# An up projection fed with x times the norm's weight, 1/rms applied at eviction, norms by logarithm, and paired fillers in a triangular inverse

## The chip, the cores and the metric

The kernel runs on one core of one Trainium2 chip. The metric is device time in microseconds of one execution of the whole step, and the median of several timed runs counts. Beside them one execution was profiled; all rows below come from that one.

## The reference, cut to what matters

One layer of a hybrid decoder is applied to 1040 prompt rows (16 learned meta tokens and 1024 prompt tokens) and 8 decode rows; the kernel carries them together as 1050 columns (two are padding). All inputs are float32.

```
def rms_norm(x, g):
    xf = x.astype(jnp.float32)
    y = xf * lax.rsqrt(jnp.mean(xf * xf, axis=-1, keepdims=True) + RMS_EPS)
    return (y * g.astype(jnp.float32)).astype(x.dtype)
...
    h = rms_norm(x, lw['norm_mix'])
    u = h @ lw['w_in']
...
    merged = jax.nn.sigmoid(g_r) * (o_r @ lw['w_br_rwkv']) + jax.nn.sigmoid(g_f) * (o_f @ lw['w_br_fox'])
    x = x + merged @ lw['w_out']
    h2 = rms_norm(x, lw['norm_ffn'])
    x = x + jnp.square(jax.nn.relu(h2 @ lw['w_ffn_up'])) @ lw['w_ffn_down']
...
    y_prompt = rms_norm(xp[:, N_META:], norm_final)
```

Between `u` and `merged` stand a recurrent branch (RWKV-7: per head a 64x64 state with a delta rule, run over time) and an attention branch with a forget bias (FoX). D_MODEL is 1024, the MLP is 4096 wide, and there are 8 heads of 64 in each branch.

## The kernel before

**Layout.** The residual x lies transposed in SBUF as 8 tiles of 128 features by 1050 columns (`XT`, k = 0 to 7). A projection makes one tile of 128 output features at a time, in three PSUM banks of 350 columns; this is called a unit here. Units alternate between slot s = 0 (banks 0 to 2) and s = 1 (banks 3 to 5), and banks 6 and 7 are left to others. Two units are a pair `v`, and its weights are loaded by SyncE into `W[:, s]`.

**Split units** (`pe_unit_split`, L273 to L286). The RWKV input projection, the branch, out, up and down projections multiply in two parts of each operand: high (rounded to float32r, by ScalarE) and low (the remainder, by VectorE). Each k needs nine matmuls (high by high, high weight by low x, low weight by high x, three banks each), so a unit has 72. ScalarE makes a unit's high weights (`act_split`, L288), VectorE its low ones (`dve_split`, L296). A unit waits for its weights, for the emptying of its slot (`evac[s]`), and, if it is given `ready`, for each k of its input.

**RMS norms** (n = 0 before the input projection, 1 before the MLP, 2 at the end). ScalarE squares a tile (L307 to L313), VectorE adds the squares up (L320 to L325), TensorE sums over partitions with three float32 matmuls by ones into banks 0 to 2 (`pe_norm`, L300), ScalarE takes the square root of all 1050 columns (`act_rms`, L315), VectorE the reciprocal (`dve_rms`, L327), and then VectorE makes each normed tile as x times weight times 1/rms (`normed`, L331). For norms 0 and 1 ScalarE and VectorE then split the tile into high and low, and the next projection waits tile by tile. For norm 2 each of the eight tiles is stored by its own DMA, in order (L784 to L786).

**The RWKV chunks.** Ten chunks of 104 columns run one after the other (`pe_chunk`). In a chunk TensorE follows an order written out by hand. It inverts a triangular matrix per head by doubling, in levels 1 to 6 (`LEVELS`, L954 to L998). Level by level: products `t1` (banks 0 and 1, both half-sets q of four heads), ScalarE copies them to `T1`, products `t2` (for each q first X times T1 into bank 2 + q, then T1 times X transposed into bank 4 + q), and VectorE subtracts these from `Xm` (L1734) and `XTr` (L1737). GpSimd meanwhile makes the next levels' masked operands (L2099). The products are 64-row or 40-row tiles, each float32 matmul being two instructions. Between these steps stand fillers (`Filler`, L334 to L352): full 128x128 float32 matmuls, two instructions each, of the FoX and gate projections. 48 fillers belong to a chunk; in the inverse one stands after `t1` and one after `t2`.

**The MLP.** Four chunks of 8 up units and 8 down units. After an up unit ScalarE empties the slot with Relu, VectorE squares, ScalarE makes the high and VectorE the low part (`act_up` L1556, `dve_up` L2051). After an out or down unit VectorE adds the banks to `XT` (`residual`, L2015 to L2020).

**Queues.** Each engine works through its instructions in order, so an instruction that waits holds all behind it; SyncE's DMA issues likewise.

## Time and profile before

| | us |
|---|---|
| median of three timed runs (2258.6 to 2265.17) | 2263.16 |
| the profiled execution | 2257.22 |
| its span, first to last instruction | 2255.4 |
| TensorE busy in it | 2101.6 (93%) |
| VectorE busy | 920.3 (41%) |
| ScalarE busy | 592.5 (26%) |
| GpSimd busy | 191.8 (9%) |

The profile lists instructions by engine (PE is TensorE's matmuls, PEld its weight loads, DVE is VectorE, ACT ScalarE, POOL GpSimd, SP SyncE) and source line. A row of the timeline is start, duration, engine, line, operation, tiles, shapes, count, and in brackets the idle time of the engine before it with what ended it. A busy TensorE is not TensorE at its peak: where matmul records overlap, the distance of their starts counts. The stretches of the execution are: norm 0 (to 64 us), RWKV input projection (to 227), preparation (to 288), ten chunks of 64.8 us each (to 925), rest of the fillers and attention (to 1260), branch and out projections (to 1458), norm 1 (to 1493), MLP (to 2226), norm 2 and the stores (to 2255).

### The profile page before, as it was taken

How to read it: one execution, taken by the hardware profiler on the slowest of the kernel's cores; microseconds unless marked ns; L12 is line 12 of the kernel's file. 1: busy time of each engine (PE TensorE's matmuls, PEld its weight loads, DVE VectorE, ACT ScalarE, POOL GpSimd, SP SyncE). 2: the span in 40 equal slices, each digit the busy share in tenths (PEclk: the TensorE clock that was granted, in tenths of full speed). 3: DMA queues.
4: the chain of work that ended last, by engine and by line, in shares of the span. 5: the costliest groups of instructions: out<-in, count | busy, mean ns of one | idle time of the engine just before them, and what ended most of it. 6: DMA issues, size and time to landing. Idle time of an engine off the chain costs nothing.

```text
span 2255.4 us, 42657 instructions
## 1 busy us (share of the span) xinstructions
PE 2101.6 (93%) x17388; PEld 1800.3 (80%) x17388; DVE 920.3 (41%) x1448; ACT 592.5 (26%) x955; POOL 191.8 (9%) x186
## 2 busy tenths in 40 slices
PE   2999899999999999998999899979999999999995
PEld 1999477777777777655566899879999999999994
DVE  5433534444433344341877663362223223212334
ACT  3213422222222222212544651232112102101210
POOL 0000022222122222001210000000000000000000
PEclk8999899999999999999999999989999999999998
DMA  3122511111102221565646362101111111111111
GB/s 119 39 84 76 222 38 48 47 47 47 37 25 55 55 66 43 143 123 183 206 167 211 132 219 94 37 29 46 47 47 46 47 46 37 46 46 46 46 37 76
DMA packets 104545, 180.96 MB, mean 80 GB/s; under 512 B 59886, under 2 KB 60206, under 8 KB 102342
## 3 DMA queue, kind: packets, MB, share of 16 engines
q1 hardware_dynamic: 102118, 170.65, 23.1%
q10 hardware_dynamic: 2304, 8.50, 1.6%
q8 instruction: 99, 1.62, 0.3%
q14 instruction: 24, 0.20, 0.0%
HBM read 145.58 MB, written 33.54 MB: 79 GB/s over the span
## 4 chain that ended last, share of the span: by engine, by line
PE 81%; DVE 8%; DMA 4%; SPq 2%; ACT 2%; issue 2%; DVEq 0%; ACTq 0%
PE ps L284 46%; PE ps L350 18%; PE ps L903 4%; PE ps L904 3%; DMA weights<-in_wu 2%; DVE arena L1713 1%; SPq L731 1%; DMA normed<-in_vp 1%; SPq L737 1%; PE ps L1020 1%; DVE normed L332 1%; PE ps L1142 1%; PE ps L1025 1%; PE ps L943 1%; PE ps L1013 1%
## 5 line engine op out<-in xcount | busy, mean ns | idle before, releaser
L350 PE MATMUL ps<-normed,weights 128*128 128x350 f32 x1344 | 446.3, 474 | 5.0 <-DMA weights<-in_wu 4.2
L284 PE MATMUL ps<-h_split,w_split 128*128 128x350 f32 x2304 | 374.9, 325 | 15.6 <-DVE h_split L2039 15.6
L284 PEld LDWEIGHTS ps<-h_split,w_split 128*128 128x128 f32 x2304 | 373.1, 190 | 17.8 <-issue 12.9
L284 PE MATMUL ps<-ff_split,w_split 128*128 128x350 f32 x2304 | 371.4, 323 | 0.0
L284 PEld LDWEIGHTS ps<-ff_split,w_split 128*128 128x128 f32 x2304 | 370.9, 189 | 0.0
L350 PEld LDWEIGHTS ps<-normed,weights 128*128 128x128 f32 x1344 | 243.2, 191 | 126.5 <-issue 14.3
L903 PEld LDWEIGHTS ps<-arena 64*64 64x64 f32 x2400 | 148.6, 135 | 46.1 <-issue 26.5
L2020 DVE TENSOR_TENSOR arena<-arena,ps 128x1050 f32 (+1 forms) x40 | 50.0, 1249 | 328.1 <-PE ps L284 328.1
L2099 POOL TENSOR_TENSOR arena<-arena,constants 64x512 f32<-64x512 f32 x120 | 132.5, 1105 | 445.6 <-DVE arena L1713 378.8
L903 PE MATMUL ps<-arena 64*64 64x64 f32 x2400 | 163.7, 220 | 1.0
L904 PE MATMUL ps<-arena 40*40 40x64 f32 x2400 | 157.5, 218 | 0.0
L294 ACT CAST w_split<-weights 128x1024 fp32r<-128x1024 f32 x78 | 81.3, 1043 | 276.8 <-PE ps L284 245.1
L284 PE MATMUL ps<-h_high,w_split 128*128 128x350 f32 x672 | 135.3, 334 | 15.4 <-DVE h_low L1593 15.4
L2055 DVE TENSOR_TENSOR squares<-squares 128x1050 f32<-128x1050 f32 x32 | 40.1, 1253 | 248.5 <-ACT squares L1561 248.5
L904 PEld LDWEIGHTS ps<-arena 40*40 40x40 f32 x2400 | 138.8, 112 | 0.0
L284 PEld LDWEIGHTS ps<-h_high,w_split 128*128 128x128 f32 x672 | 114.4, 192 | 19.9 <-issue 13.9
L298 DVE TENSOR_TENSOR w_split<-weights,w_split 128x1024 fp32r<-128x1024 f32 x78 | 95.1, 1219 | 78.3 <-ACT w_split L294 78.3
L1734 DVE TENSOR_TENSOR arena<-arena,ps 104x256 f32<-104x256 f32 (+1 forms) x100 | 41.9, 419 | 190.3 <-PE ps L904 184.2
L1561 ACT ACTIVATE squares<-ps 128x1050 f32<-128x1050 f32 x32 | 33.5, 1048 | 259.5 <-PE ps L284 259.5
L1411 ACT COPY arena<-ps 104x256 f32<-104x256 f32 (+1 forms) x120 | 44.6, 372 | 160.1 <-PE ps L904 116.0
L1862 DVE CUSTOM_DVE_ANT_0 arena<-ps,arena 104x416 f32<-104x416 f32 (+3 forms) x152 | 67.7, 492 | 36.6 <-PE ps L1187 36.6
L284 PE MATMUL ps<-mg_high,wb_split 128*128 128x350 f32 x384 | 73.9, 328 | 5.2 <-DVE wb_split L298 5.2
(282 smaller groups left out, 2424.7 us busy)
## 6 DMA issues: line engine op xcount, KB each, us to landing
weights<-in_wu SPq DMA_DIRECT2D x122, 512.0 KB, 3.5
normed<-in_vp SPq DMA_DIRECT2D x64, 260.0 KB, 4.5
normed<-in_kp SPq DMA_DIRECT2D x64, 256.0 KB, 4.9
arena<-chunk_dram SPq DMA_DIRECT2D x10, 1248.0 KB, 6.9
arena<-gate_dram SPq DMA_DIRECT2D x16, 525.0 KB, 4.0
chunk_dram<-arena SPq DMA_DIRECT2D x12, 520.0 KB, 4.0
chunk_dram<-fox SPq DMA_DIRECT2D x12, 520.0 KB, 3.8
arena<-samp_dram SPq DMA_DIRECT2D x10, 512.0 KB, 9.2
```

Of the source, the lines that this page charges most:

```text
L284: last = pe.matmul(PS[:, 3 * s + g, 0:G], ws[s][wh][:, k * P:(k + 1) * P], x[xh][:, k, g * G:(g + 1) * G], start=(k == 0 and wh + xh == 0) ...
L294: act.copy(of[0][s][0], W[:, s]).then_inc(w_hi[s], 1)
L298: dve.tensor_tensor(of[0][s][1], W[:, s], of[0][s][0], ALU.subtract).then_inc(w_split[s], 1)
L350: last = self.pe.matmul(PS[:, 6 + m % 2, 0:G], W[:, s, k * P:(k + 1) * P], HT[:, k, g * G:(g + 1) * G], start=(k == 0), stop=(k == KT - 1))
L903: pe.matmul(PS[top, bank, at], a[top], b[top], start=True, stop=True)
L904: return pe.matmul(PS[low, bank, at], a[low, 0:HR], b[low], start=True, stop=True)
L1411: ch_act.done(act.copy(quad(T1, q)[part], PS[part, q, 0:4 * HB]), f"t1_{lv}_{q}")
L1734: done(dve.tensor_tensor(quad(Xm, q)[part], quad(Xm, q)[part], PS[part, 2 + q, 0:4 * HB], ALU.subtract), f"x_{lv}_{q}_x")
L1862: dve.tensor_tensor_reduce(Sm[u % 3][0:C, e, lo:hi].rearrange("p b t -> p (b t)"), PS[0:C, 2 * (n % 2) + e, (lo - CUTS[c][0]) * C:(hi - CU ...
L2020: dve.tensor_tensor(dst, dst, grp(s), ALU.add).then_inc(evac[s], 1)
L2055: dve.tensor_tensor(RL[s], RL[s], RL[s], ALU.mult).then_inc(ff_raw, 1)
L2099: ch_pool.done(pool.tensor_tensor(Bm[lv % 2][part, :, 0:n], MB[part, :, 0, part], mask.unsqueeze(1).to_broadcast([n, NH, n]), ALU.mult), f ...
```

## The change

**Norms.** `act_rms` takes the logarithm group by group (three instructions of 350 columns, the weight 1/D and the epsilon in it), and then one exponential of -0.5 times it over 1050 columns; that is 1/rms, and VectorE's reciprocal goes. `pe_norm` signals after each of its three groups; norms 0 and 1 write banks 6 and 7 (group 2 waits until group 0 is read), norm 2 banks 0 to 2.

**Norm 1 and the MLP.** As soon as an out tile k is added to `XT`, ScalarE writes `HS[0][k]`, the high part of x times the norm's weight, and VectorE the low part. The first up unit follows the last out unit directly; the three sums over partitions are put into it, two groups ahead of its k = 5 and one ahead of k = 7. 1/rms is applied where an up unit is emptied, by VectorE (maximum with 0, times 1/rms), then ScalarE squares and makes the high part, and VectorE the low part. ReLU and the scale commute, because 1/rms is positive. Buffers of the split operands move to other places.

**Norm 2.** VectorE makes tiles 0 to 5. ScalarE multiplies tiles 6 and 7 of `XT` by the weight ahead of time, and GpSimd multiplies them by 1/rms. The stores are issued in the order 0, 1, 6, 2, 3, 7, 4, 5.

**Inverse.** The products that change X get a signal of their own (`t2x`) and come first for both q, then the other products; VectorE subtracts in that order. The next level's `t1` waits for X alone, and `t2x` for X transposed. The two fillers of a level stand together between `t1` and `t2`.

```diff
@@ pe_norm, act_rms, dve_rms
-        def pe_norm(pe, n):
+        def norm_out(n, g):
+
+            return PS[:, g if n == 2 else 6 + g % 2, 0:G]
+
+        def pe_norm(pe, n, groups=range(NG)):
             sqsum = norms[n][1]
-            pe.wait_ge(sq_added, KT * (n + 1))
-            for g in range(NG):
-                last = pe.matmul(PS[:, g, 0:G], ones, sqsum[:, g * G:(g + 1) * G], start=True, stop=True)
-            last.then_inc(ssum_ready, 1)
+            for g in groups:
+                pe.wait_ge(sq_added, KT * (n + 1))
+                if g == 2 and n < 2:
+                    pe.wait_ge(rms_ready[n], 1)
+                pe.matmul(norm_out(n, g), ones, sqsum[:, g * G:(g + 1) * G], start=True, stop=True)\
+                  .then_inc(ssum_ready[n], 1)
...
-            act.wait_ge(ssum_ready, n + 1)
-            act.activation(g3(norms[n][2]), grp(0), ACT.Sqrt, scale=1.0 / D,
-                           bias=par[:, V_EPS:V_EPS + 1]).then_inc(rms_ready, 1)
+            rstd = norms[n][2]
+            for g in range(NG):
+                act.wait_ge(ssum_ready[n], g + 1)
+                act.activation(rstd[:, g * G:(g + 1) * G], norm_out(n, g), ACT.Ln, scale=1.0 / D,
+                               bias=par[:, V_EPS:V_EPS + 1]).then_inc(rms_ready[n], 1)
+            act.wait_ge(rms_ready[n], NG)
+            act.activation(rstd, rstd, ACT.Exp, scale=-0.5).then_inc(rms_ready[n], 1)
...
-            dve.wait_ge(rms_ready, n + 1)
-            order(dve.reciprocal(norms[n][2], norms[n][2]))
+            dve.wait_ge(rms_ready[n], NG + 1)
@@ sync: the stores
-            for k in range(KT):
-                sp.wait_ge(h_ready, 2 * KT + k + 1)
+            for k in (0, 1, 6, 2, 3, 7, 4, 5):
+                if k < N_DVE:
+                    sp.wait_ge(h_ready, 2 * KT + k + 1)
+                else:
+                    sp.wait_ge(out_made, k - N_DVE + 1)
                 sp.dma_start(A["o_y"][:, k, :], HT[:, k, :]).then_inc(out_stored, 16)
@@ tensor: the inverse
-                            wait(ch_dve, f"x_{lv - 1}_{q}_xt")
+                            wait(ch_dve, f"x_{lv - 1}_{q}_x")
...
-                    fill.run(1)
+                    fill.run(2)
                     for q in range(2):
                         wait(ch_act, f"t1_{lv}_{q}")
+                        if lv > 1:
+                            wait(ch_dve, f"x_{lv - 1}_{q}_xt")
...
+                        ch_pe.done(last, f"t2x_{lv}_{q}")
+                    for q in range(2):
                         for j in range(4):
                             last = by_halves(4 + q, j, T1, XTr, 4 * q + j)
                         ch_pe.done(last, f"t2_{lv}_{q}")
-                    fill.run(1)
@@ tensor: the MLP's start
-            pe.wait_ge(evac[0], V_FF0 - PV_FILL)
-            pe_norm(pe, 1)
-            pe.wait_ge(rms_ready, 2)
-            pe_unit_split(pe, V_FF0, 0, halves(HS), lambda k: pe.wait_ge(h_ready, KT + 1 + k))
-            pe_unit_split(pe, V_FF0, 1, halves(HS))
+            def summed(k):
+                pe.wait_ge(h_ready, KT + 1 + k)
+                if k == 5:
+                    pe_norm(pe, 1, (0, 1))
+                if k == 7:
+                    pe_norm(pe, 1, (2,))
+
+            pe_unit_split(pe, V_FF0, 0, HS, summed)
+            pe_unit_split(pe, V_FF0, 1, HS)
@@ scalar: out projection, up units, the end
+            for k in range(KT):
+                j, s = divmod(k, 2)
+                act_split(act, j + (V_OUT0 + 1), s, of=BRO)
+                act.wait_ge(evac[s], j + (V_OUT0 - PV_FILL + 1))
+                act.activation(HS[0][:, k], XT[:, k, :], ACT.Identity,
+                               scale=par[:, V_NF + k:V_NF + k + 1]).then_inc(h_hi, 1)
+                act_square(act, 1, k, s)
             act_rms(act, 1)
...
-                        act.activation(g3(RL[s]), grp(s), ACT.Relu).then_inc(evac[s], 1)
                         act_split(act, KT * c + j + (V_FF0 + 1), s)
+                        act.wait_ge(evac[s], KT * c + j + (V_FF0 - PV_FILL + 1))
+                        act.activation(RL[s], RL[s], ACT.Square).then_inc(ff_raw, 1)
...
+                    if 2 * j + s >= N_DVE:
+                        k = 2 * j + s
+                        act.wait_ge(sq_ready, 2 * KT + k + 1)
+                        act.activation(XT[:, k, :], XT[:, k, :], ACT.Identity, scale=par[:, V_NL + k:V_NL + k + 1])\
+                           .then_inc(out_scaled, 1)
@@ vector: out projection, up units, the end
+            for k in range(KT):
+                j, s = divmod(k, 2)
+                residual(j, k + (2 * V_OUT0 + 1), s)
+                dve_split(dve, j + (V_OUT0 + 1), s, of=BRO)
                 dve.wait_ge(h_hi, k + 1)
+                dve.scalar_tensor_tensor(HS[1][k], XT[:, k, :], par[:, V_NF + k:V_NF + k + 1],
+                                         HS[0][:, k].bitcast(F32), ALU.mult, ALU.subtract).then_inc(h_ready, 1)
+                dve_add_square(dve, 1, k, s)
+            dve_rms(dve, 1)
...
-                        dve.tensor_tensor(RL[s], RL[s], RL[s], ALU.mult).then_inc(ff_raw, 1)
+                        dve.scalar_tensor_tensor(g3(RL[s]), grp(s), 0.0, rstd1, ALU.max, ALU.mult)\
+                           .then_inc(evac[s], 1)
...
-            for k in range(KT):
+            for k in range(N_DVE):
                 normed(dve, 2, k, V_NL, HT[:, k, :]).then_inc(h_ready, 1)
@@ gpsimd: the end
+            pool.wait_ge(rms_ready[2], NG + 1)
+            for k in range(N_DVE, KT):
+                pool.wait_ge(out_scaled, k - N_DVE + 1)
+                pool.tensor_tensor(HT[:, k, :], XT[:, k, :], norms[2][2], ALU.mult).then_inc(out_made, 1)
```

## Rows read from the trace of the kernel before

**Rows 1.** The page: busy time by engine, and the chain that ended last, by engine.
```profile
PE 2101.6 (93%) x17388; PEld 1800.3 (80%) x17388; DVE 920.3 (41%) x1448; ACT 592.5 (26%) x955; POOL 191.8 (9%) x186
...
PE 81%; DVE 8%; DMA 4%; SPq 2%; ACT 2%; issue 2%; DVEq 0%; ACTq 0%
```
**Rows 2.** The waits of TensorE: us in total, times, longest.
```profile
PE ps L304 <- DVE arena L325: 35.3, 2, 31.5
PE ps L284 <- DVE h_split L2039: 15.6, 5, 11.9
```
**Rows 3.** The timeline of norm 0: ScalarE's root, VectorE's reciprocal and next step.
```profile
35.33 1.14 ACT L317 ACTIVATE arena<-ps,params 128x1050 f32<-128x1050 f32 x1 [3.39 <-PE ps L304]
36.50 6.72 DVE L329 RECIPROCAL arena<-arena 128x1050 f32<-128x1050 f32 x1 [5.19 <-ACT arena L317]
43.25 1.22 DVE L298 TENSOR_TENSOR w_split<-weights,w_split 128x1024 fp32r<-128x1024 f32 x1
```
**Rows 4.** The timeline of ScalarE in a chunk: a 350-column bank, Ln, Exp's table.
```profile
657.52 0.45 ACT L363 COPY fox<-ps 128x350 f32 x1 [3.21 <-PE ps L350]
...
663.05 0.30 ACT L1420 ACTIVATE arena<-arena,params 104x8 f32<-104x8 f32 x1 [3.77 <-DVE arena L1771]
663.37 1.28 ACT L1423 ACT_TABLE_LOAD   x1
```
**Rows 5.** The timeline of TensorE in the inverse: four fillers, then level 1's single ones.
```profile
620.36 2.62 PE L350 MATMUL ps<-normed,weights 128*128 128x350 f32 x8
622.91 0.27 PE L903 MATMUL ps<-arena 64*64 64x64 f32 x1
...
625.98 0.27 PE L903 MATMUL ps<-arena 64*64 64x64 f32 x1
...
627.78 0.28 PE L903 MATMUL ps<-arena 64*64 64x64 f32 x2
627.99 0.86 PE L350 MATMUL ps<-normed,weights 128*128 128x350 f32 x2
628.77 0.27 PE L903 MATMUL ps<-arena 64*64 64x64 f32 x1
```
**Rows 6.** The timeline of VectorE at the same place: its first subtraction of level 1.
```profile
627.18 0.42 DVE L1734 TENSOR_TENSOR arena<-arena,ps 104x256 f32<-104x256 f32 x1 [7.32 <-PE ps L904]
```
**Rows 7.** The timeline around norm 1: last out tile, first up unit, its emptying.
```profile
1457.73 1.25 DVE L2020 TENSOR_TENSOR arena<-arena,ps 128x1050 f32<-128x1050 f32 x1 [7.96 <-PE ps L284]
...
1476.77 7.18 PE L284 MATMUL ps<-h_split,w_split 128*128 128x350 f32 x27 [11.94 <-DVE h_split L2039]
...
1496.09 1.05 ACT L1561 ACTIVATE squares<-ps 128x1050 f32<-128x1050 f32 x1 [3.46 <-PE ps L284]
```
**Rows 8.** The chain that ended last, in order of time: start, us, what.
```profile
1492.75 732.93 PE ps L284 x4554
```
**Rows 9.** Stretches: busy PE, PEld, DVE, ACT, POOL (instructions), granted clock, DMA share, GB/s.
```profile
1457.00:1477.00 20.00, 4.24 (x12) 2.16 (x11) 14.39 (x8) 6.57 (x6) 0.00 (x0) 0.71 0.09 26
1500.00:1594.00 94.00, 94.00 (x586) 94.00 (x585) 28.95 (x24) 22.45 (x22) 0.00 (x0) 1.00 0.14 50
```
**Rows 10.** The timeline of norm 2: reciprocal and the eight normed tiles.
```profile
2233.99 6.72 DVE L329 RECIPROCAL fox<-fox 128x1050 f32<-128x1050 f32 x1 [4.65 <-ACT fox L317]
2240.74 9.87 DVE L332 SCALAR_TENSOR_TENSOR normed<-arena,params,fox 128x1050 f32<-128x1050 f32 x8
```
**Rows 11.** The DMA of the stores, from 2242.3 to 2253.5 us.
```profile
DMA packets 1138, 4.29 MB, mean 383 GB/s; under 512 B 117, under 2 KB 117, under 8 KB 1137
```
**Rows 12.** The timeline of GpSimd and VectorE at a chunk's start, both reading SBUF.
```profile
669.31 1.44 POOL L2106 TENSOR_TENSOR arena<-arena 128x416 f32 x1 [32.45 <-ACT arena L1428]
670.02 1.17 DVE L1699 TENSOR_TENSOR arena<-arena 128x416 f32<-128x416 f32 x1
671.02 1.10 POOL L2109 TENSOR_TENSOR arena<-arena  x1 [0.28 <-POOL arena L2106]
...
672.60 0.59 DVE L1702 TENSOR_TENSOR arena<-arena 128x416 f32<-128x416 f32 x1
```
**Rows 13.** Groups of GpSimd by line and shape: busy us, mean ns.
```profile
L2124 POOL TENSOR_TENSOR arena<-arena,constants 104x1040 f32<-104x1040 f32 x4 | 9.6, 2410 | 0.0
```

More of the change, by code:

```diff
@@ L325, in dve_add_square, with dve_rms @@
             dve.tensor_tensor(sqsum, sqsum, sq[:, slot], ALU.add).then_inc(sq_added, 1)
[L327 to L329 removed]
+        def dve_rms(dve, n):
+            dve.wait_ge(rms_ready[n], NG + 1)
         def normed(dve, n, k, gain, dst):
@@ L988, in pe_chunk @@
                     ch_pe.done(last, f"t1_{lv}_{q}")
-                fill.run(1)
+                fill.run(2)
                 for q in range(2):
@@ L997, in pe_chunk @@
                     ch_pe.done(last, f"t2_{lv}_{q}")
-                fill.run(1)
                 def u_out(e, p):
@@ L1589, in _ @@
                 dve_add_square(dve, 0, k, k % 2)
-            dve_rms(dve, 0, order)
+            dve_rms(dve, 0)
             def low_half0(k):
@@ L1724, in _, with moved @@
                 for lv in LEVELS:
+                    def moved(bank, part, n):
+                        return PS[part, bank, 0:4 * HB].rearrange("p (a b) -> p a b", a=4)[:, :, 0:n]
+                    if lv < N_LV - 1:
+                        part = slice(0, C) if lv < N_LV - 2 else top
+                        for q in range(2):
+                            wait(ch_pe, f"t2x_{lv}_{q}")
+                            done(dve.tensor_tensor(quad(Xm, q)[part], quad(Xm, q)[part], PS[part, 2 + q, 0:4 * HB],
+                                                   ALU.subtract), f"x_{lv}_{q}_x")
                     for q in range(2):
@@ L2080, in _ @@
                         dve_split(dve, V_FF0 + KT * FF_CH - KT // 2 + j + 1, s)
-            dve_rms(dve, 2, order)
-            for k in range(KT):
+            dve_rms(dve, 2)
+            for k in range(N_DVE):
                 normed(dve, 2, k, V_NL, HT[:, k, :]).then_inc(h_ready, 1)
```

122 lines of the change are left out of this document (41 added, 81 removed).

## The prediction

> **What bounds the kernel now.** I read the page first, then TensorE's waits, then the timeline at the four places that the change touches. TensorE is busy 93% of the span and is 81% of the chain that ended last [rows 1], so an edit is worth something only where TensorE stands still, where it pays for something beside its multiplications, or ahead of its first and behind its last one. TensorE's waits name the standstills: 35.3 us in two waits of L304 (the sum of squares), the larger part of it the loading of inputs at the start, which the change leaves alone, and 15.6 us of the first up unit for its split input [rows 2]. In the MLP itself nothing is to be had: 94 us of 94 are busy at a granted clock of 1.00 [rows 9], and 4554 matmuls in 732.93 us [rows 8] are 0.1609 us each, so 11.59 us per unit of 72.
>
> **Norm 0.** Before: root from 35.33 to 36.47, reciprocal to 43.22, next step at 43.25 [rows 3]. After: the last of three sums ends where it ended (group 2's extra wait is for a logarithm of group 0, which is finished before TensorE reaches group 2, two sums later). Then a logarithm of 350 columns out of PSUM, 0.45 by the copy of such a bank; then Exp's table, which the trace loads between Ln and Exp, 1.28 [rows 4]; then Exp over 1050 columns, 1.05 to 1.14 by the ScalarE passes of that size [rows 3, 7]. 35.33 + 0.45 + 1.28 + 1.1 = 38.2: **5.0 us less**. What comes behind, VectorE making tiles one by one, is unchanged and moves as a whole. Bounds: 4.4 (the logarithm as dear as 1.0) and 6.3 (no table to load). The Trainium skill, "ScalarE: Activation LUTs", section "Table sets: the hidden batching unit", says that one set holds ln and exp and that Ln followed by Exp needs one load. Here the trace shows a load of 1.28 between the two, so the measurement decides; by the page norms 0 and 2 would each give 1.3 us more, an estimate that is no part of my sum.
>
> **The inverse.** TensorE waits for no one there; it pays for changing between full fillers and 64-row products. From the last product of level 1 (the second of the two from 627.78, at 627.84) to the next product (628.77) one filler takes 0.93. Four fillers take 622.91 - 620.36 = 2.55 up to the first product, one takes 628.77 - 627.99 = 0.78: so each further filler in a run costs 0.59 [rows 5]. Moving the second filler of a level beside the first saves 0.93 - 0.59 less the distance of two products, 0.03 (1.80 us for 64): 0.31. That happens in levels 1 to 5 of ten chunks; in level 6 the moved filler only leaves a run of three for a run of two, nothing gained. 50 x 0.31 = **15.5 us less**. The cover that goes away: t1 of the next level now follows the products at once and waits for X. The products that change X come first, 16 for q = 0, that is 0.46 us. VectorE began 1.20 after the first of 32 products (627.18 against 625.98) [rows 5, 6], so 0.29 after the last; it would begin at 0.75 and end at 1.17 for q = 0, and at about 1.63 for q = 1. t1 starts at 1.84 and needs q = 1 only at 2.30, so 0.6 us of slack are left for both. X transposed has two fillers and t1 to arrive. If that slack were wrong by 0.6 us I would still keep it at zero cost; bounds 10 to 16.
>
> **Norm 1.** Before: the last out unit ends at 1457.7, the first up unit begins at 1476.77, limps behind VectorE tile by tile and is emptied at 1496.09 [rows 7]; from there the MLP runs evenly to 1492.75 + 732.93 = 2225.68 [rows 8]. So the MLP ends 768.0 after the last out unit. After: 64 units x 11.59 = 741.6, without a break, plus six float32 matmul instructions for the sums. Priced as fillers of the same size these are 1.3 for two sums and 0.7 for one, and some 0.15 on entry each: 2.3. 768.0 - 743.9 = **24.1 us less**. Is the first up unit fed? Its k = 7 needs the last out tile: VectorE's addition (1.25 from 1457.73), weight split (1.22), low part (1.3) and square sum (1.25) end 5.1 us after the unit. k = 5 with the first sums comes 5 x 9 x 0.161 = 7.2 us after it, so nothing waits, 2 us of slack. 1/rms: the last sum is issued at 11.7, then Ln, table and Exp, 2.8 in all as above: 14.7, while the up unit ends at 13.9. VectorE empties its slot a microsecond late, and TensorE wants that slot only 11.6 later. In the old gap the granted clock was 0.71, between the two levels of 1.2 and 2.4 GHz, TensorE having stood still for 11.94 us before 1476.77 [rows 7, 9]; without the gap the cause goes, and the price of that clock is within the 768.0 already. Bounds: 22 (each entry of a sum twice as dear) and 25.
>
> **Up units.** The emptying moves from ScalarE to VectorE, the square the other way. Four passes of 1.05 to 1.31 and one weight split between them still end within about 6 us of a unit's end, under the 11.59 of the next one. The first down unit wants the last tile at its k = 7, 10.1 us after. Out units get a pass more on ScalarE and one on VectorE, 5 us of 11.6. All this is hidden: 0. It would cost something only if the chain of a unit passed 10 us.
>
> **Norm 2.** Logarithm and exponential in place of root and reciprocal: 5.0 us less up to 1/rms, as in norm 0 (Ln's own table can be loaded while the sums still run). Behind it stand eight tiles in 9.87 us, 1.23 each [rows 10], and their stores. These are bound by the DMA: 4.29 MB at 383 GB/s, 11.2 us for eight [rows 11], 1.3 to 1.4 a tile, more than VectorE's 1.23. So two tiles fewer on VectorE give nothing, and the question is what GpSimd's two cost. At a chunk's start VectorE's product took 1.17 beside GpSimd's, and 0.59 when it had SBUF to itself [rows 12]: it stood until GpSimd was through. The Trainium skill, "SBUF — State Buffer", section "Who interferes with whom", says that a VectorE instruction with two SBUF inputs and a GpSimd instruction that reads SBUF exclude each other for a whole instruction; the trace agrees (1.17 against 0.59), and it speaks against this edit. GpSimd needs 2.41 for 1040 columns [rows 13]. If they take turns, VectorE's tile 1 is ready 2.3 later than before and tile 2 4.6 later, the DMA runs dry twice, and the last store ends 2.9 later than in the DMA-bound case. Bounds: 0 (no exclusion) and 5.9 (GpSimd comes only after VectorE's six tiles, at 7.4 + 2.4 = 9.8, and the store of tile 6, third in SyncE's order, holds the five behind it). I take turns, since in [rows 12] each engine got in behind the other: 5.0 - 2.9 = **2.1 us less**.
>
> **The sum.** 5.0 + 15.5 + 24.1 + 0 + 2.1 = 46.7 us. Against the profiled execution, 2257.22, that is 2210.5. The timed runs lie 1.4 to 8 us above that execution, their mean at 2262.3; less 46.7 that is 2215.6, and I say 2215 for the median.
>
> **Rivals.**
> No exclusion at the end: the gain there is 5.0, in all 49.6, time 2213. For it: ScalarE's scaling ahead leaves GpSimd a plain product of two operands. Against it: [rows 12].
> GpSimd starved: the end costs 0.9 more than before, in all 43.7, time 2219.
> The pairs in the inverse give nothing, because t1 then stands for X instead of paying for a filler's switch: 31.2, time 2231. For it: the filler was the cover of VectorE's subtraction. Against it: the 0.6 us of slack.
> The norm does not leave the path: the sums within the first up unit are reached before the squares are added, or the split comes late. With the price of one tile's chain, 5 us, and its clock at half for as long again: 36, time 2226. Against it: 2 us of slack.
> Slower than before: the same exposure of X in the inverse, but larger. VectorE's subtraction there runs beside GpSimd's masks, of the kind that stretched 0.59 to 1.17; if it were held until late, each of the 50 levels pays whatever exceeds the 0.6 of slack plus the 0.31 saved. The 31.2 us of the other parts are gone when each level loses 0.62 us net, so from a delay of about 1.5 us at all five levels of all chunks; at 2 us it is 23 us slower than that point, 2286. Against it: the subtraction reads PSUM and one SBUF tile, and GpSimd has work in three of five levels only.
> That the change does nothing: the reciprocal and the gap are on the chain by their rows, so only if all three slacks above were wrong at once.
>
> **How the numbers follow.** Forecast (turns at the end) 0.55; no exclusion 0.15; starved 0.10; late norm 0.07; pairs without gain 0.07; slower 0.03; no effect 0.03. Range: the sum's ends are 4.4 + 10 + 22 - 0.9 = 35.5 and 6.3 + 16 + 25 + 6.3 = 53.6; taken from the fastest timed run (2258.6) and from the slowest (2265.17) and without their unlikeliest corners: 2206 to 2226. About 0.3% is what a measurement of this kernel can tell from no change. Faster 0.94, within 0.3% 0.03, slower 0.03.
>
> **What would show it.** Norm 0: Exp ends near 38.2 and the first split matmul comes near 43.2. Inverse: a chunk lasts 63.2 in place of 64.8, one run of two fillers (four instructions) per level, no wait of TensorE for L1734's successor. Norm 1: no RECIPROCAL, three runs of L304's successor inside the first up unit, 11.6 us between all units, granted clock 1.00 throughout. End: GpSimd's two products of 2.4 beside VectorE passes longer than 1.3 and a DMA rate that drops to zero between stores; if those passes keep 1.23, the exclusion is refuted. The prediction is wrong if chunks last over 64 us, or if the first up unit ends more than 15 us after the last out unit.

## The result, and the profile after

The changed kernel takes **2210.86 us** (median of 4 runs, 2208.32 to 2212.23), the kernel before 2260.88 in the runs beside it: a ratio of **0.978, 95% interval 0.9755 to 0.9797**. The forecast was 2215, with 2206 to 2226 as its range and "faster" at 0.94. The profiled execution of after took 2210.57 us, its span is 2208.8 against 2255.4, so the span fell by 46.6 where the sum said 46.7. That agreement is partly luck: one term was too small by 5, and a stretch that the change does not touch was longer by 7 in this execution.

For the split by place I took eight marks that both traces have and subtracted their times (us):

```
stretch                                     before     after   difference
start to first split matmul (norm 0)         48.23     43.31     -4.92
  to chunk 0                                236.33    235.12     -1.21
ten chunks                                  640.48    619.93    -20.55
  to the branch projection (attention)      337.77    344.47     +6.70
branch and out projection                   194.92    193.71     -1.21
last out tile to last down tile (norm 1)    767.98    744.61    -23.37
  to norm 2's first normed tile              15.04      9.82     -5.22
  to the end of the span                     14.64     17.79     +3.15
span                                       2255.39   2208.76    -46.63
```

The attention stretch lay between 335.9 and 347.2 us in the profiles of this study, whatever was changed (337.77 in before, 335.96 and 347.17 with experiments below that leave it alone). TensorE waits there 5.7 to 8.8 us for pages of keys and values from the DMA in every trace. What varies most is one more wait, for a filler's weights: 5.7 us in after and 4.2 in before, and where it is 0.2 or less the stretch takes 335.9 to 339.6. So the stretch hides or adds some 10 us of any single span, and verdicts below go by the stretch that an edit touches.

The page of after, by engine (busy us, share of the span, instructions), answers to [rows 1]:

```profile
PE 2074.8 (94%) x17388; PEld 1794.9 (81%) x17388; DVE 891.6 (40%) x1435; ACT 609.1 (28%) x970; POOL 197.1 (9%) x188
```

TensorE's waits of after (us in total, times, longest) answer to [rows 2]:

```profile
PE ps L314 <- DVE arena L339: 35.3, 2, 31.5
```

L314 is the old L304 (the sums of squares). The total of 35.3 us in two waits is that of [rows 2], but the waits are not the same two. In the kernel before they were the loading of inputs (31.5) and norm 1 (3.8), and norm 2 had 3.8 in a row of its own; now they are the loading and norm 2, and norm 1's wait is gone. The row of 15.6 us for the split input of the first up unit has no successor.

**Norm 0**, timeline of after, answering to [rows 3]: start, us, engine, line, operation.

```profile
35.35 0.55 ACT L329 ACTIVATE arena<-ps,params 128x350 f32<-128x350 f32 x1 [0.61 <-PE ps L314]
35.92 1.28 ACT L332 ACT_TABLE_LOAD   x1
37.22 1.08 ACT L332 ACTIVATE arena<-arena 128x1050 f32<-128x1050 f32 x1
38.33 1.22 DVE L302 TENSOR_TENSOR w_split<-weights,w_split 128x1024 fp32r<-128x1024 f32 x1 [7.00 <-ACT arena L332]
```

The logarithm of the last bank begins where the root began (35.35 against 35.33), and VectorE goes on at 38.33 instead of 43.25. The table load that was read from a chunk [rows 4] is there, with the same 1.28.

**The inverse**, timeline of TensorE in after at levels 1 and 2, answering to [rows 5], and VectorE's subtractions at the same place, answering to [rows 6]:

```profile
608.41 0.22 PE L921 MATMUL ps<-arena 64*64 64x64 f32 x1
608.55 1.45 PE L363 MATMUL ps<-normed,weights 128*128 128x350 f32 x4
609.93 0.27 PE L921 MATMUL ps<-arena 64*64 64x64 f32 x1
```

```profile
610.73 0.89 DVE L1751 TENSOR_TENSOR arena<-arena,ps 104x256 f32<-104x256 f32 x2 [7.65 <-PE ps L922]
```

The two fillers of a level now stand together, as a run of four instructions. From the start of the last product ahead of them (608.41) to the start of the first one behind them (609.93) it takes 1.52 us, where a single filler took 0.93. Both subtractions of X run from 0.80 to 1.69 us after the first product; the forecast had 0.75 and 1.63.

**Norm 1**, timeline of after, answering to [rows 7]:

```profile
1436.33 0.65 PE L288 MATMUL ps<-h_high,wb_split 128*128 128x350 f32 x3
1436.53 1.25 DVE L2040 TENSOR_TENSOR arena<-arena,ps 128x1050 f32<-128x1050 f32 x1 [6.65 <-PE ps L288]
...
1443.56 1.34 PE L314 MATMUL ps<-arena,constants 128*128 128x350 f32 x4
...
1447.63 0.75 PE L314 MATMUL ps<-arena,constants 128*128 128x350 f32 x2
...
1450.29 1.08 ACT L332 ACTIVATE arena<-arena 128x1050 f32<-128x1050 f32 x1
...
1451.85 1.25 DVE L2057 SCALAR_TENSOR_TENSOR squares<-ps,arena 128x1050 f32<-128x1050 f32 x1 [10.35 <-ACT arena L332]
```

The chain that ended last, in order of time (start, us, what), answers to [rows 8]:

```profile
1447.79 0.59 PE ps L314 x2
1448.38 732.74 PE ps L288 x4545
```

A stretch of 14 us from the first up unit's start, with the columns of [rows 9]:

```profile
1436.00:1450.00 14.00, 14.00 (x85) 13.37 (x84) 4.86 (x4) 7.14 (x8) 0.00 (x0) 1.00 0.12 39
```

The first up unit's first product (1436.33) begins before VectorE adds the last out tile (1436.53). The sums lie inside the unit as runs of four and two instructions, TensorE is busy 14.00 of 14.00 us at a granted clock of 1.00, and 1/rms comes at 1451.4, when only VectorE's emptying waits for it. In [rows 7] TensorE stood for 11.94 us here, at 0.71 [rows 9].

**Norm 2**, timeline of after, answering to [rows 10]:

```profile
2187.99 0.55 ACT L329 ACTIVATE arena<-ps,params 128x350 f32<-128x350 f32 x1 [0.61 <-PE ps L314]
2188.56 1.28 ACT L332 ACT_TABLE_LOAD   x1
2189.86 1.08 ACT L332 ACTIVATE arena<-arena 128x1050 f32<-128x1050 f32 x1
2190.97 11.45 DVE L345 SCALAR_TENSOR_TENSOR normed<-arena,params 128x1050 f32<-128x1050 f32 x6 [6.18 <-ACT arena L332]
2191.01 5.41 POOL L2150 TENSOR_TENSOR normed<-arena 128x1050 f32<-128x1050 f32 x2 [982.81 <-ACT arena L332]
```

The DMA of after from 2194 us to the end of the span, in 40 slices, over the stores of [rows 11]:

```profile
GB/s 0 0 0 136 397 431 420 68 0 0 0 79 397 397 386 375 409 386 375 420 397 431 386 431 409 420 409 420 397 409 431 397 431 420 409 420 329 0 0 0
```

Six passes of VectorE now take 11.45 us; eight took 9.87 [rows 10]. One by one, VectorE's first two need 3.55 and 3.09 and the other four 1.3, GpSimd's two 2.39 and 3.05. The two engines take turns as the forecast said, and the store rate falls to zero once, between the first store and the second.

### The profile page after: what moved, and what is told of

The parts are those of the page before. It is cut to its first block, busy times and chain, and to the rows that moved or that the text cites. A ratio compares the mean times of both kernels' runs of the same rounds, so it can differ in the third digit from the quotient of the medians.

```text
span 2208.8 us, 42564 instructions
## 1 busy us (share of the span) xinstructions
PE 2074.8 (94%) x17388; PEld 1794.9 (81%) x17388; DVE 891.6 (40%) x1435; ACT 609.1 (28%) x970; POOL 197.1 (9%) x188
## 3 DMA queue, kind: packets, MB, share of 16 engines
q1 hardware_dynamic: 102118, 170.65, 24.1%
## 4 chain that ended last, share of the span: by engine, by line
PE 67%; issue 19%; POOL 4%; DMA 3%; DVE 3%; SPq 2%; ACT 1%; ACTq 0%; POOLq 0%; DVEq 0%
PE ps L288 40%; PE ps L363 13%; PE ps L921 3%; POOL arena L2102 3%; PE ps L922 3%; DMA weights<-in_wu 2%; DMA normed<-in_kp 1%; SPq L753 1%; SPq L747 1%; PE ps L1103 1%; PE ps L1040 1%; PE ps L1033 1%; PE ps L1045 1%; DVE arena L1882 1%; POOL arena L2109 1%
## 5 line engine op out<-in xcount | busy, mean ns | idle before, releaser
L363 PE MATMUL ps<-normed,weights 128*128 128x350 f32 x1344 | 430.1, 468 | 6.8 <-DMA weights<-in_wu 5.7
L288 PE MATMUL ps<-h_high,wb_split 128*128 128x350 f32 x1536 | 290.5, 324 | 0.0
L288 PE MATMUL ps<-ff_high,wb_split 128*128 128x350 f32 x1536 | 290.0, 323 | 0.0
L298 ACT CAST wb_split<-weights 128x1024 fp32r<-128x1024 f32 x88 | 92.1, 1046 | 599.6 <-PE ps L288 592.1
L288 PEld LDWEIGHTS ps<-ff_high,wb_split 128*128 128x128 f32 x1536 | 255.2, 189 | 0.0
L288 PEld LDWEIGHTS ps<-h_high,wb_split 128*128 128x128 f32 x1536 | 254.7, 189 | 0.4
L288 PE MATMUL ps<-ff_low,wb_split 128*128 128x350 f32 x768 | 165.5, 323 | 0.0
L288 PEld LDWEIGHTS ps<-ff_low,wb_split 128*128 128x128 f32 x768 | 131.1, 189 | 0.0
L2057 DVE SCALAR_TENSOR_TENSOR squares<-ps,arena 128x1050 f32<-128x1050 f32 x32 | 40.0, 1251 | 220.7 <-PE ps L288 210.3
L302 DVE TENSOR_TENSOR wb_split<-weights,wb_split 128x1024 fp32r<-128x1024 f32 x88 | 107.1, 1218 | 8.8 <-ACT wb_split L298 7.2
```

Of the source, the lines that this page charges most:

```text
L288: last = pe.matmul(PS[:, 3 * s + g, 0:G], ws[s][wh][:, k * P:(k + 1) * P], tile_of(x[xh], k)[:, g * G:(g + 1) * G], start=(k == 0 and wh + ...
L298: act.copy(of[0][s][0], W[:, s]).then_inc(w_hi[s], 1)
L302: dve.tensor_tensor(of[0][s][1], W[:, s], of[0][s][0], ALU.subtract).then_inc(w_split[s], 1)
L363: last = self.pe.matmul(PS[:, 6 + m % 2, 0:G], W[:, s, k * P:(k + 1) * P], HT[:, k, g * G:(g + 1) * G], start=(k == 0), stop=(k == KT - 1))
L2057: dve.scalar_tensor_tensor(g3(RL[s]), grp(s), 0.0, rstd1, ALU.max, ALU.mult)\
```

## The experiments

Each edit is against the changed kernel unless it is said otherwise. Medians of the runs are given with the ratio to the kernel before in the same session.

### 1. The end: who delays whom

All eight tiles back on VectorE:

```diff
-N_DVE = 6
+N_DVE = 8
-            for k in (0, 1, 6, 2, 3, 7, 4, 5):
+            for k in range(KT):
```

> The changed kernel, but VectorE makes all eight tiles of norm 2 and the stores go out in order 0 to 7; GpSimd has no part in it. Theory (VectorE and GpSimd exclude each other, the stores are bound by the DMA): VectorE's passes fall from 3.55, 3.09 and 1.30 back to 1.23 to 1.31 each, and from the end of 1/rms to the end of the span it takes 14.7 us, as before the change, in place of 17.85; the whole is 3 us faster than the changed kernel, 2207.7. Rival (GpSimd's help is worth its price, or it is free): 14.7 becomes 17.5 or more, the time 2211 or above.

And GpSimd kept, but 1/rms written to PSUM for VectorE, so that VectorE reads one operand from SBUF and one from PSUM:

```diff
+            if n == 2:
+                act.activation(grp(1), g3(rstd), ACT.Exp, scale=-0.5).then_inc(rms_ready[n], 1)
+                act.wait_ge(rms_ready[n], NG + 1)
             act.activation(rstd, rstd, ACT.Exp, scale=-0.5).then_inc(rms_ready[n], 1)
...
-                normed(dve, 2, k, V_NL, HT[:, k, :]).then_inc(h_ready, 1)
+                dve.scalar_tensor_tensor(g3(HT[:, k, :]), g3(XT[:, k, :]), par[:, V_NL + k:V_NL + k + 1],
+                                         grp(1), ALU.mult, ALU.mult).then_inc(h_ready, 1)
```

> The changed kernel, but ScalarE writes 1/rms for norm 2 twice, first into PSUM for VectorE, then into SBUF for GpSimd, so that VectorE's six passes read one operand from SBUF and one from PSUM while GpSimd still reads two from SBUF. Theory (what VectorE and GpSimd contend for is the second SBUF operand): VectorE's passes are 1.2 to 1.3 us each beside GpSimd's of 2.4, the stores run without a break, and 1/rms to the end takes 14.7 to 15.0. Rival (any two passes at once hold each other up, or GpSimd's waits do): some VectorE passes stay at 3 us and the end at 17 to 18.

The timeline of the first:

```profile
2187.66 9.87 DVE L345 SCALAR_TENSOR_TENSOR normed<-arena,params 128x1050 f32<-128x1050 f32 x8 [6.84 <-ACT arena L332]
2189.00 8.89 SPq L805 DMA_DIRECT2D out_o_y<-normed  x8
```

and of the second:

```profile
2188.19 7.40 DVE L2089 SCALAR_TENSOR_TENSOR normed<-arena,params,ps 128x1050 f32<-128x1050 f32 x6 [6.05 <-ACT ps L333]
2189.34 4.42 POOL L2154 TENSOR_TENSOR normed<-arena 128x1050 f32<-128x1050 f32 x2 [986.78 <-ACT arena L335]
```

From VectorE's first normed tile to the end of the span the first takes 13.82 us, the second 13.85, the changed kernel 17.79. (The expected 14.7 was the kernel before's own value; see norm 2 below.) VectorE's six passes are back at 1.23 each with GpSimd running beside them, as soon as their second operand lies in PSUM, and GpSimd's two fall from 5.41 to 4.42. So the loss is the exclusion over SBUF, and nothing that ScalarE or the order of the stores does. The Trainium skill, "SBUF — State Buffer", section "Who interferes with whom", says that a VectorE instruction with two SBUF inputs and a GpSimd instruction that reads SBUF shut each other out for whole instructions; both traces agree, 11.45 with two such inputs against 7.40 with one. Without the exclusion GpSimd's help is still worth nothing, 13.85 against 13.82, because the stores are bound by the DMA [rows 11].

By time: 2203.54 us (2199.44 to 2208.61), ratio 0.9756 [0.9734, 0.9778], and 2205.14 us (2203.84 to 2210.87), ratio 0.9768 [0.9744, 0.9792]. **All tiles on VectorE is the better version by the stretch that it touches:** 3.97 us less at the end than the changed kernel. The whole times show it faster than the kernel before; against the changed kernel they decide nothing. The medians lie 7.3 apart, but the intervals of the ratios overlap, and in the two profiles the attention stretch alone differs by 6.2 (338.3 against 344.5).

### 2. The inverse: how much, and which part of it

The old inverse put back (order of products and subtractions, single fillers), all else as changed; and the new inverse alone, in the kernel before:

> The changed kernel with the inverse as before: two single fillers per level, products and subtractions in the old order. Theory: a chunk lasts 64.8 us again in place of 62.7, ten chunks are 20.5 us longer, the time is 2231. Rival (the 15.5 us of the prediction are the inverse's, and 5 us of the chunks come from other parts of the change): 64.2 per chunk, the time 2226.

> The kernel before with the new inverse alone (early X and paired fillers). Theory: ten chunks take 620 us in place of 640.5, all other stretches as before, the time 20 us under the kernel before, 2240. Rival (part of the chunks' gain comes from the norms or from the moved buffers): 625 us for ten chunks, 15 us under the kernel before, 2245.

The ten chunks took 641.27 us with the old inverse and 619.97 with the new one alone, against 640.48 and 619.93 in before and after. So the inverse's gain is the same in either surrounding, and it adds to the other parts. How exact is such a difference? From the start of one chunk to the start of the next, the second to the ninth chunk of one trace take the same time, to 0.01 us: 64.77 in before and with the old inverse put back, 62.72 in after and with the new one alone, so 2.05 us a chunk. The first chunk alone is uneven: in traces that have the same chunks as after it takes 63.94 to 64.89 us, and so the sum of ten lies between 619.9 and 620.9. A difference of less than 1 us between two sums of ten says nothing; the length of a later chunk does.

Times: 2229.66 (ratio 0.9861 [0.9838, 0.9885]) and 2235.92 (0.9898 [0.9872, 0.9925]). The 15.5 of the forecast is refuted: 5 us are missing in it.

The new inverse does two things, and each was run without the other. Fillers in pairs, but the old order, where t1 of the next level waits for VectorE's X only (the lines shown are against the kernel with the old inverse):

```diff
                         ch_pe.done(last, f"t1_{lv}_{q}")
-                    fill.run(1)
+                    fill.run(2)
...
                         ch_pe.done(last, f"t2_{lv}_{q}")
-                    fill.run(1)
```

> The changed kernel with paired fillers, but the products in the old order (for each half-set q first the one that changes X, then the one that changes X transposed) and VectorE's subtractions likewise; the next level's t1 still waits for X alone. Theory (the early X is the cover that makes the pair free): X of q = 1 is ready 2.6 us after the products begin and is wanted at 2.3, so TensorE stands 0.3 us in each of 50 levels: 13 to 16 us slower than the changed kernel, 2224 to 2227. Rival (pairing alone does it): no wait in the levels, 2211.

and the new order, but single fillers:

```diff
-                    fill.run(2)
+                    fill.run(1)
...
                         ch_pe.done(last, f"t2_{lv}_{q}")
+                    fill.run(1)
```

> The changed kernel with the products and subtractions in the new order (early X), but the two fillers of a level apart again, one after t1 and one after the second products. Theory (the gain is the saved switch between fillers and 64-row products, and the order only makes it possible): ten chunks take 637 to 641 us, as in the kernel before, the time 2229 to 2231. Rival (the early X gives the gain by itself): 620 us for ten chunks, the time 2211.

Ten chunks: 643.99 and 638.51 us; one later chunk: 65.13 and 64.57. Pairs without the early products are dearer than single fillers in the old order (64.77), and by 24.1 us in ten chunks dearer than the changed kernel, more than the 13 to 16 expected: the longer run of fillers is saved, but TensorE then stands for X. TensorE's waits show where it stands longest, after level 5, in each of ten chunks; at levels 1 to 4 the products of a level take 3.28 us in place of 2.94, in smaller pieces.

```profile
PE ps L1002 <- DVE arena L1748: 6.7, 10, 0.7
```

Against the old inverse the new order without pairs gives 0.20 us a chunk, 2.0 in ten (the sums of ten differ by 2.8, of which 0.8 lie in the uneven first chunk), and pairs on top of it 1.85 a chunk, 18.5 in ten. Times: 2232.22 (0.9874 [0.9851, 0.9898]) and 2227.24 (0.9856 [0.983, 0.9883]). So the forecast's reason for moving the products that change X ahead was right: it is what makes the pairs pay. But why should the order alone give 2.0, when no wait of TensorE in the levels has gone?

### 3. The 2 us that were no part of the plan

The block of 32 products (L952) ahead of the inverse is shorter in after, 3.94 us from its first product to its last, against 4.14 in before. VectorE's masks, four passes of 104x832, take the products out of PSUM, and the block's second half waits until the first two passes have emptied its banks. That wait of TensorE is a row in both traces (us in total, times, longest), which the prediction passed over; of before:

```profile
PE ps L934 <- DVE arena L1713: 8.8, 20, 0.7
```

and of after:

```profile
PE ps L952 <- DVE arena L1732: 6.0, 10, 0.6
```

VectorE's groups by line and shape (busy us, mean ns, then idle time ahead of them), of before:

```profile
L1713 DVE TENSOR_TENSOR arena<-ps,constants 104x832 f32<-104x832 f32 x40 | 40.9, 1023 | 5.3 <-PE ps L934 0.5
```

the changed kernel:

```profile
L1732 DVE TENSOR_TENSOR arena<-ps,constants 104x832 f32<-104x832 f32 x40 | 41.0, 1024 | 1.9 <-PE ps L952 0.2
```

and the changed kernel with the old inverse put back:

```profile
L1727 DVE TENSOR_TENSOR arena<-ps,constants 104x832 f32<-104x832 f32 x40 | 41.0, 1025 | 6.0 <-PE ps L949 1.3
```

The passes are the same 1.02 us; the idle time between them is not. The records of VectorE's own queue in the trace, which these views do not count, show what stands between two passes:

```
with the old inverse put back               in the changed kernel
608.848  1025 ns  mask pass                 595.835  1024 ns  mask pass
608.873    40 ns  ALU_OP (register)         595.848    40 ns  ALU_OP (register)
609.911    40 ns  ALU_OP (register)         596.352    21 ns  EVENT_SEMAPHORE
609.995  1026 ns  mask pass                 596.893  1024 ns  mask pass
```

VectorE's chunks are a loop, so it compares semaphores with c x (steps of a chunk) + number, worked out in a register. The second register operation is that of the next wait, for TensorE. It can only run after the wait for the pass before it, and the next pass waits for it. In the changed kernel it is missing, and the wait for TensorE (EVENT_SEMAPHORE) is taken while the pass before still runs. TensorE has 48 steps per chunk there, because the early products got ten steps of their own, and VectorE has 48 as well; in the kernel before it was 38 and 48. My theory: with equal counts the value that VectorE needs for TensorE's step has been worked out already, for an earlier step of its own. To test it, no work is moved; only empty steps are added. First ten to TensorE with the old inverse, ahead of the products, then one to the changed kernel:

```diff
-        ch_pe = Steps(sem("ch_pe"), ["nat_k", "nat_b", "nat_v"]
+        ch_pe = Steps(sem("ch_pe"), ["nat_k", "nat_b"] + [f"pad_{i}" for i in range(10)] + ["nat_v"]
```

> The kernel with the inverse as it was before (single fillers, old order), and only the count of TensorE's steps in a chunk changed: 10 empty steps bring it from 38 to 48, the count that VectorE has; the step of the third transposed block counts eleven at once. No work is moved. In the traces so far VectorE's passes between the products and the inverse follow each other at 0.81 and 1.15 us where TensorE has 38 steps, and between two passes stands an operation of VectorE's queue on a register (0.04 us, the value that the next wait compares with), which is missing where TensorE has 48 steps as VectorE has, and the distances are 0.73 and 1.06. Theory (the wait's value is computed anew for each wait where the counts of two engines differ): the block of 32 products falls from 4.14 to 3.94 us, the ten chunks from 641.3 to 638.5-639.5 us. Rival (the order of the products and subtractions does it): block 4.14, ten chunks 641 to 641.6.

> The changed kernel with one empty step more for TensorE in each chunk, 49 in place of 48; nothing else. Theory (equal counts save VectorE's register operation): VectorE's distances go back to 0.81 and 1.15, the block of 32 products to 4.14, the ten chunks from 619.9 to 621.5-622.5 us. Rival (the order does it): block 3.94, ten chunks 619.9 to 620.4.

The second came out as the theory says: one empty step, 49 against 48, and a later chunk goes from 62.72 to 62.91 us (ten of them from 619.93 to 622.47), VectorE's distances from 0.73 between copies and 1.06 to 1.09 between masks to 0.81 and 1.15, the block to 4.14 in all chunks but the first. The first missed: 641.16 us, a later chunk 64.83, distances unchanged. Its group, and its idle time (5.4):

```profile
L1730 DVE TENSOR_TENSOR arena<-ps,constants 104x832 f32<-104x832 f32 x40 | 40.9, 1023 | 5.4 <-PE ps L952 0.6
```

and that of the second (5.8):

```profile
L1735 DVE TENSOR_TENSOR arena<-ps,constants 104x832 f32<-104x832 f32 x40 | 40.9, 1024 | 5.8 <-PE ps L955 1.0
```

The miss had a reason that could be tried. Empty steps ahead of the products raise their numbers from 3 to 6 to 13 to 16, past what VectorE has worked out by then. So the same ten steps were put behind the products:

```diff
-                      + ["u", "y", "s", "yt"])
+                      + [f"pad_{i}" for i in range(10)] + ["u", "y", "s", "yt"])
```

> The old inverse again, with TensorE's 10 empty steps behind the products instead of ahead of them, so that the products keep their numbers (3 to 6 of 48) as in the changed kernel. Theory: the register operation between VectorE's passes goes only where the counts are equal (48 and 48) and the number waited for is one that VectorE has already worked out for an earlier step of its own; then the distances are 0.73 and 1.06 us, the block of 32 products takes 3.94, and the ten chunks 639 to 639.5 us in place of 641.3. Rival (with the old order of the products it stays): 0.81 and 1.15, 4.14 and 641 to 641.6.

The same group in this kernel:

```profile
L1730 DVE TENSOR_TENSOR arena<-ps,constants 104x832 f32<-104x832 f32 x40 | 41.0, 1024 | 1.9 <-PE ps L952 0.2
```

Idle 1.9 again, the block 3.95 in a later chunk where it was 4.14, the ten chunks 638.47 us, half a microsecond less than expected. A later chunk takes 64.57 us, with the old order of all work exactly what the new order gave without pairs, and 0.20 less than with 38 steps (64.77). So the new order itself gives nothing, and the 2.0 are the register operation: ten times the 0.20 by which the block is shorter.

That a value is shared between the two engines' steps can also be counted: VectorE's queue has 914 register operations (ALU_OP) in the trace with the old inverse, 1014 in the one with 49 steps against 48, and 724 in the three with equal counts: the changed kernel and both versions with ten empty steps. The version that missed has no more of them than the one that came out; they stand elsewhere, between the passes. So the number alone does not decide, the place does. The times, 2234.17 and 2213.51 us for the first two (0.9882 [0.9844, 0.9921] and 0.979 [0.9753, 0.9828]) and 2222.34 for the third (one run), contain the attention stretch and decide nothing here.

### 4. The norms: what the logarithm is worth where

Root and reciprocal put back in all three norms:

```diff
-                act.activation(rstd[:, g * G:(g + 1) * G], norm_out(n, g), ACT.Ln, scale=1.0 / D,
+                act.activation(rstd[:, g * G:(g + 1) * G], norm_out(n, g), ACT.Sqrt, scale=1.0 / D,
...
-            act.wait_ge(rms_ready[n], NG)
-            act.activation(rstd, rstd, ACT.Exp, scale=-0.5).then_inc(rms_ready[n], 1)
...
+            dve.wait_ge(rms_ready[n], NG)
+            dve.reciprocal(norms[n][2], norms[n][2]).then_inc(rms_ready[n], 1)
```

> The changed kernel with square root on ScalarE and reciprocal on VectorE in place of logarithm and exponential, in all three norms. Theory: norms 0 and 2 lie open, each 6.7 us of reciprocal against 2.4 of table and Exp, so the first split matmul comes at 47.6 in place of 43.3 and 1/rms of norm 2 is 4.3 us later; norm 1 is hidden, because TensorE wants the first up unit's banks only 11.6 us after that unit ends, and the stretch from the last out tile to the last down tile stays at 744.6; the time is 2219.5. Rival (norm 1's chain is on the path after all): that stretch grows by 4 as well, the time is 2224.

The first split matmul comes at 47.55 instead of 43.31, norm 2's first tile 14.74 instead of 9.82 after the last down tile, and the stretch of norm 1 and the MLP is 744.61 in both, to the hundredth. Norms 0 and 2 are open, and the whole chain of norm 1 is hidden: there the logarithm buys nothing. The time, 2214.96 us (0.9801 [0.9778, 0.9825]), is 4.1 above after where the two stretches make 9.2; in its profile the attention stretch gave back 8.6 (335.9).

All of norm 1's sums ahead of the first up unit, so that unit starts only when the last tile has been added:

```diff
             def summed(k):
                 pe.wait_ge(h_ready, KT + 1 + k)
-                if k == 5:
-                    pe_norm(pe, 1, (0, 1))
-                if k == 7:
-                    pe_norm(pe, 1, (2,))
+            pe_norm(pe, 1)
             pe_unit_split(pe, V_FF0, 0, HS, summed)
```

> The changed kernel with all three sums of norm 1 ahead of the first up unit, so that TensorE waits for the last square sum before that unit, but not for 1/rms. Theory: it stands 5 us, the sums take 3 us at the lower clock in place of 1.75 within the unit, and the unit starts at that clock: the stretch from the last out tile to the last down tile is 752 to 755 in place of 744.6, the time 2219 to 2221; so some 8 to 10 of the 23.4 us are the early start, and the rest is what the tile-by-tile norm cost. Rival (nearly all is the early start): 760 or more.

Its timeline at that place:

```profile
1436.94 3.62 PE L314 MATMUL ps<-arena,constants 128*128 128x350 f32 x6 [5.06 <-DVE arena L339]
...
1440.09 0.96 PE L288 MATMUL ps<-h_high,wb_split 128*128 128x350 f32 x3
```

The timeline shows that TensorE stands for 5.06 us and the sums take 3.62 instead of 1.75; the stretch is 751.56, 6.95 longer, just under the 752 to 755 expected. So 7.0 of norm 1's 23.4 us belong to hiding the sums in the unit; the other 16.4, by subtraction, to not waiting for 1/rms and the tiles made from it. (This one is read by its profile, whose execution took 2213.32 us. The other three runs took 2217.79, 3244.50 and 4225.35 us, so their median says nothing.)

## Why the prediction was right, and where it was not

**Norm 0: right.** 4.92 us against 5.0, within 4.4 to 6.3. The logarithm of a bank took 0.55, where a copy of such a bank had given 0.45; the rest is as the rows said. Putting root and reciprocal back, group by group, cost 4.24; most of the other 0.7 is the root over 1050 columns at once (1.14) against the last logarithm (0.55).

**The inverse: right in mechanism and sign, too small in size**, 20.55 against 15.5 and outside its bounds of 10 to 16. The term that was mis-sized is "0.93 - 0.59 less the distance of two products, 0.03: 0.31, in levels 1 to 5" with its 50 x 0.31 = 15.5. Three things stand differently. Levels 1 to 4 gave 0.335 each, as 4.65 us of a level became 4.31: 13.4 in ten chunks against 12.4. Level 5 gave 0.507 instead of 0.31: its neighbour, level 6, has products of 64 rows by 40, which begin in after while the last ones of level 5 still run, and I had taken the levels as alike (this is read from the trace; no run took it away). That is 5.1 against 3.1. And 2.0 come from the masks ahead of the inverse, VectorE's register operation; no view that I read has a row of it, though TensorE's wait for those masks had one. 13.4 + 5.1 + 2.0 = 20.5, and the run with equal steps and the old order shows the split: 0.20 and 1.85 us a chunk. The error that lay deepest is the upper bound: it was set at 16 because only fillers were counted, while the diff also changed the list of steps, and each wait of a loop is worked out from that list.

The slack for X of 0.6 us held: the changed inverse shows no wait of TensorE for the subtraction. The run with pairs in the old order shows the other side of it: 24.1 us more in the ten chunks (2.0 of them the register operation), which is more than the whole gain.

**Norm 1: right.** 23.37 against 24.1, within 22 to 25. The six instructions of the sums cost 1.75, less than the 2.3 of the sum (13.33 us from the first up unit's start to the next one's, less 11.58). What took the gain back is the term "Up units: 0": a down unit lasts 11.62 where it was 11.586, an up unit 11.58 to 11.61. Over 64 units that is some 1.3 us more than the sum's 741.6. The operands of the split moved to other places in SBUF, but no run tested that, so its cause stays open. The claims on 1/rms and on the clock are in the rows: Exp ended at 1451.37, VectorE's emptying alone waited for it, and the granted clock is 1.00 through both units.

**Norm 2: right in both halves, the turns in another order.** 5.22 less up to the first tile (5.0). That the two agree to 0.2 is partly luck: in runs that leave this stretch as it is in after it takes 8.81 to 10.49 us. TensorE has stood still for 3.83 us when it begins the three sums over partitions. At the lower end (the old inverse with equal steps) the granted clock was 1.00 through them and TensorE was busy 2.01 us with them; at the upper end (all tiles on VectorE) the mean granted clock was 0.62 and they took 3.68; in after it was 0.66, and 3.02. Why it fell in one run and not in the other is not shown. Behind it come the turns between the engines. I wrote 2.9 for those; the stretch shows 3.15 against the kernel before, and 3.95 against the runs with an undisturbed tail (13.82 to 13.85), since the stores of the kernel before were 0.8 slower in its profiled execution. The rivals "no exclusion" and "GpSimd starved" are both refuted. GpSimd got in at once. Its record begins 0.04 us behind VectorE's, but by the durations it went first: its pass took 2.39, no more than beside VectorE's PSUM version (2.41), and VectorE's took 3.55. The forecast had VectorE first: tile 0 on time, tile 1 late by 2.3, tile 2 by 4.6, and the stores running dry twice. In after tile 0 was already late by 2.2 us and tile 1 by 4.0, and the stores ran dry once. That giving tiles to GpSimd loses was in the sum, and the experiment without it gives those 4 us back.

**The sum.** 4.9 + 20.5 + 23.4 + 5.2 - 3.2 is 50.9, against 46.7. The timed medians differ by 50.0 us, the profiled spans by 46.6. The difference of the profiles is short because of the attention stretch (+6.7), partly made up by the stretches around it. So the forecast lay 4 us too high in time, by the inverse, and its range held.

The rivals that would have made it slow (X exposed in the inverse, norm 1 late) did not decide, but the first of them is real: it lies one reordering away.

## What to carry to other kernels

Cost a moved instruction by what stands on both sides of it: here a pair of fillers pays only because the products that the next step needs were moved ahead of it, and it costs more than it saves if they are not. An engine that is idle is no help where it reads the same memory as the busy one and the stage is bound by the stores anyway: ask first which resource ends the stage, then how many operands each helper takes from it. And where a loop's waits are computed, the counting of steps is part of the path: compare the idle time between equal instructions on both sides of a change, not only their durations.

## What the runs showed that I had not expected

- A wait of VectorE against a computed value cost 0.06 to 0.09 us per pass where the value had to be worked out after the pass before it: masks at 1.15 us distance in place of 1.06 to 1.09 and copies at 0.81 in place of 0.73, 0.20 us a chunk and 2.0 in ten. Equal step counts remove it (a chunk of 64.57 us against 64.77), one empty step too many brings it back (62.91 against 62.72), and so does raising the numbers of the awaited steps (64.83).
- Two engines that exclude each other over SBUF took strict turns, instruction by instruction: VectorE 3.55 and 3.09 beside GpSimd 2.39 and 3.05. GpSimd's first pass, which went first, lost nothing (2.41 without the exclusion), its second one did (2.05), and the pair rose from 4.42 to 5.41. One operand in PSUM ended it.
- Root and reciprocal or logarithm in norm 1 made no hundredth of a microsecond of difference (744.61 us either way): the MLP's stretch repeats to that precision, so a change of 7 us (751.56) or of 0 there is read from one profile.
